# Third mixer's q,k convolution computed in the second mixer's stage

## The reference

```python
cqkv, gdnc1 = causal_conv(dqkv, gdnc0, prm['gdn_conv_w'][i])   # 4 taps along time
cqkv = jax.nn.silu(cqkv)
cq, ck, cv = jnp.split(cqkv, [GDN_H * GDN_DK, 2 * GDN_H * GDN_DK], axis=-1)
q = l2norm(heads(cq, GDN_H)) * GDN_DK ** -0.5
k = l2norm(heads(ck, GDN_H))
v = heads(cv, GDN_H)
```

## Time and profile before

| | |
|---|---|
| median of 3 runs | 2600.65 us (2597.46 to 2604.7) |
| profiled execution, its own time | 2596.66 us |
| span in its profile | 2594.9 us |
| PE busy | 2399.1 us (92%) |
| DVE, ACT, POOL busy | 1639.1 (63%), 1074.1 (41%), 181.1 (7%) |
| chain that ended last | PE 72%, DVE 17%, issue 6%, ACT 4% |

### The profile page before, as it was taken

The page is one execution under the profiler, slowest core; times in us unless marked ns, Lnnn a source line. Parts: engine busy times, 40 slices in busy tenths (PEclk is TensorE's granted clock), DMA queues, the critical chain, the costliest instruction groups (busy, mean ns, idle before and its releaser), DMA issues.

```text
span 2594.9 us, 38245 instructions
## 1 busy us (share of the span) xinstructions
PE 2399.1 (92%) x14436; PEld 2069.6 (80%) x14436; DVE 1639.1 (63%) x2112; ACT 1074.1 (41%) x1450; POOL 181.1 (7%) x247
## 2 busy tenths in 40 slices
PE   8899898899999899899798997999999999999996
PEld 6788778876899888789687866787887878878786
DVE  4554853743665454457636633778787887878776
ACT  4332311321333334324122220566666666667662
POOL 0212111201000001202012010000000000000000
PEclk8999898998999989999898988899999999999998
DMA  5323311322444333234112320898898978889871
GB/s 197 105 87 134 131 66 41 111 82 98 152 163 163 127 130 106 95 134 142 54 50 83 110 73 32 325 327 289 300 329 297 335 284 303 319 296 332 291 278 64
DMA packets 122566, 456.43 MB, mean 176 GB/s; under 512 B 14056, under 2 KB 14474, under 8 KB 120018
## 3 DMA queue, kind: packets, MB, share of 16 engines
q1 hardware_dynamic: 118818, 432.66, 47.5%
q0 software_dynamic: 3632, 22.12, 2.4%
HBM read 443.72 MB, written 11.00 MB: 175 GB/s over the span
## 4 chain that ended last, share of the span: by engine, by line
PE 72%; DVE 17%; issue 6%; ACT 4%; POOL 1%; DVEq 0%; DMA 0%; SPq 0%; ACTq 0%; POOLq 0%
PE ps L726 7%; PE ps L728 7%; PE ps L727 7%; PE ps L773 6%; DVE weights_low L2255 4%; PE ps L1293 4%; PE ps L1295 4%; PE ps L1294 4%; PE ps L1315 3%; PE ps L1316 3%; PE ps L1317 3%; PE ps L1266 3%; PE ps L767 2%; DVE arena L1889 2%; PE ps L808 1%
## 5 line engine op out<-in xcount | busy, mean ns | idle before, releaser
L726 PE MATMUL ps<-u_high,tiles_high 128*128 128x288 f32 x1688 | 526.0, 312 | 17.5 <-DVE tiles_low L1718 17.5
L727 PE MATMUL ps<-u_low,tiles_high 128*128 128x288 f32 x1688 | 513.0, 304 | 0.0
L728 PE MATMUL ps<-u_high,tiles_low 128*128 128x288 f32 x1688 | 511.1, 303 | 0.0
L1718 DVE TENSOR_TENSOR tiles_low<-ring,tiles_high 128x1024 fp32r<-128x1024 f32 x238 | 298.1, 1255 | 201.6 <-ACT tiles_high L1374 200.2
L726 PEld LDWEIGHTS ps<-u_high,tiles_high 128*128 128x128 f32 x1688 | 332.1, 197 | 26.7 <-issue 24.6
L2255 DVE TENSOR_TENSOR weights_low<-expert_ring,weights_high 128x1024 fp32r<-128x1024 f32 x288 | 334.5, 1219 | 5.2 <-ACT weights_high L1627 2.0
L727 PEld LDWEIGHTS ps<-u_low,tiles_high 128*128 128x128 f32 x1688 | 332.6, 197 | 0.5
L728 PEld LDWEIGHTS ps<-u_high,tiles_low 128*128 128x128 f32 x1688 | 332.2, 197 | 0.0
L1374 ACT ACTIVATE tiles_high<-ring 128x1024 fp32r<-128x1024 f32 x238 | 250.6, 1054 | 170.9 <-DMA ring<-in_stream 81.0
L1293 PE MATMUL ps<-weights_high,u_high 128*128 128x512 f32 (+1 forms) x768 | 297.6, 388 | 22.9 <-DVE weights_low L2255 22.3
L2255 DVE TENSOR_TENSOR weights_low<-ring,weights_high 128x1024 fp32r<-128x1024 f32 x240 | 280.2, 1218 | 43.2 <-ACT weights_high L1627 42.1
(11 more groups left out here) (381 smaller groups left out, 3290.2 us busy)
## 6 DMA issues: line engine op xcount, KB each, us to landing
ring<-in_stream SPq DMA_DIRECT2D x530, 512.0 KB, 4.2
expert_ring<-in_stream SPq DMA_DIRECT2D x288, 512.0 KB, 5.6
arena<-in_state POOLq DMA_DIRECT2D x8, 1024.0 KB, 5.1
state_s<-arena POOLq DMA_DIRECT2D x8, 1024.0 KB, 4.3
const<-in_const SPq DMA_DIRECT2D x1, 2052.5 KB, 12.0
arena<-in_const POOLq DMA_DIRECT2D x2, 832.0 KB, 4.9
h<-in_x SPq DMA_DIRECT2D x1, 1152.0 KB, 5.0
y<-acc POOLq DMA_DIRECT2D x1, 1152.0 KB, 4.4
```

Source lines behind the costliest of these rows:

```text
L726: mm(out, hi[k], uh[:, k, :], start=k == 0, stop=False)
L727: mm(out, hi[k], ul[:, k, :], start=False, stop=False)
L728: last = mm(out, lo[k], uh[:, k, :], start=False, stop=k == KD - 1)
L1718: tt(t_low[:, q % HELD, :], ring[:, (t % RING) * TILE:(t % RING + 1) * TILE], t_high[:, q % HELD, :].bitcast(F32), ALU.subtract).then_inc( ...
```

## The change

Blocks 0 to 3 of the third mixer's convolution (q and k) move into the second mixer's stage, with buffers of their own (`cbuf_early`, `ctan_early`) beside the retention's decay table. VectorE's `conv` is split into `conv_taps` and `conv_finish`, ScalarE's tanh into `conv_tanh`. The remaining four rounds of the third mixer now handle two slots each, the squares come first and the norm stands in the third of the four rounds. TensorE's sums of squares come after two slots instead of five. The convolution of the fourth mixer is written in the new functions with the same order as before.

The buffers, and TensorE's `gdn`:

```diff
+EARLY_CONV = 4
...
             ret_dec = carve(4 * PAIR)
+            cbuf_early = carve(640).rearrange("p (a c) -> p a c", a=2)
+            ctan_early = carve(640).rearrange("p (a c) -> p a c", a=2)
...
-                for s in range(5):
+                for s in range(2):
                     fill(L, GDN, s)
...
                 last.then_inc(qksum_ps, 1)
-                for s in range(5, 8):
+                for s in range(2, 8):
                     fill(L, GDN, s)
```

ScalarE's `core`, `out_norm` and the new `conv_gdn`:

```diff
                     fill(L, n, slot + hh)
+                    if n == RET and hh == 3:
+                        conv_tanh(L, GDN, 0)
                 if n != GLA:
                     take_o(HEADS[n] - 2)
                     take_o(HEADS[n] - 1)
+                if n == RET:
+                    conv_tanh(L, GDN, 1)
...
                 fill(L, n, slot)
+                if n == RET:
+                    conv_tanh(L, GDN, 2)
                 act.wait_ge(osum_ps, m + 1)
...
-                for s in range(slot + 1, NSLOT[n]):
+                fill(L, n, slot + 1)
+                if n == RET:
+                    conv_tanh(L, GDN, 3)
+                for s in range(slot + 2, NSLOT[n]):
                     fill(L, n, s)
...
+            def conv_gdn(L):
+
+                act.wait_ge(conv_ready, 14 * L + 4)
+                A(tmp4, cv[:, 0:4, :], ACT.Square).then_inc(qksq_ready, 1)
+                for i, b in enumerate(range(EARLY_CONV, NCONV[GDN])):
+                    if i > 0:
+                        fill(L, GDN, 2 * i - 2)
+                        fill(L, GDN, 2 * i - 1)
+                    conv_tanh(L, GDN, b)
+                    if b == 5:
                         act.wait_ge(qksum_ps, L + 1)
                         A(rs4, ps_t[:, M:M + 4, 0:TOK], ACT.Sqrt, bias=C("eps")).then_inc(qkrt_ready, 1)
+                fill(L, GDN, 6)
+                fill(L, GDN, 7)
```

VectorE's `scores`, `out_norm` (the first place there is behind the two gate products) and the new `conv_gdn`:

```diff
                     fill(L, n, slot + hh)
+                    if n == RET and hh >= 2:
+                        conv_taps(L, GDN, hh - 2)
+                        if hh == 3:
+                            conv_finish(L, GDN, 0)
...
+                if n == RET:
+                    conv_taps(L, GDN, 2)
+                    conv_finish(L, GDN, 1)
                 fill(L, n, slot)
                 dve.wait_ge(ort_ready, m + 1)
...
                 dve.wait_ge(o_final, m + 1)
+                if n == RET:
+                    conv_taps(L, GDN, 3)
+                    conv_finish(L, GDN, 2)
                 fill(L, n, slot + 1)
                 state(L, n)
+                if n == RET:
+                    conv_finish(L, GDN, 3)
                 for s in range(slot + 2, NSLOT[n]):
                     fill(L, n, s)
...
+            def conv_gdn(L):
+
+                for i, b in enumerate(range(EARLY_CONV, NCONV[GDN])):
+                    conv_taps(L, GDN, b)
+                    if i > 0:
+                        conv_finish(L, GDN, b - 1)
+                        fill(L, GDN, 2 * i - 2)
+                        fill(L, GDN, 2 * i - 1)
+                    if b == 6:
+                        qk_norm(L)
+                conv_finish(L, GDN, NCONV[GDN] - 1)
+                fill(L, GDN, 6)
+                fill(L, GDN, 7)
```

More of the change, by code:

```diff
@@ L1503, in decays, with conv_tanh, conv_ssd @@
                 A(egp[:, 0:q, :], egp[:, 0:q, :], ACT.Exp).then_inc(eg_ready, 1)
[L1505 to L1517, removed]
+            def conv_tanh(L, n, b):
+                c = 14 * L + CONV0[n] + b
+                act.wait_ge(convsum_ready, c + 1)
+                if c - 1 > 0:
+                    act.wait_ge(conv_ready, c - 1)
+                taps, t = scratch_of(n, b)
+                A(t[:, 0:312], taps[:, 0:312], ACT.Tanh).then_inc(ctan_ready, 1)
+            def conv_gdn(L):
[7 more added lines that the diff above has]
+                    if b == 5:
                         act.wait_ge(qksum_ps, L + 1)
                         A(rs4, ps_t[:, M:M + 4, 0:TOK], ACT.Sqrt, bias=C("eps")).then_inc(qkrt_ready, 1)
-                fill(L, n, NCONV[n] - 1)
+                fill(L, GDN, 6)
+                fill(L, GDN, 7)
+            def conv_ssd(L):
+                for b in range(NCONV[SSD]):
+                    if b > 0:
+                        fill(L, SSD, b - 1)
+                    conv_tanh(L, SSD, b)
+                fill(L, SSD, NCONV[SSD] - 1)
             def gla(L):
@@ L1925, in qk_norm @@
                 dve.wait_ge(qk_ready, L + 1)
-            def conv(L, n):
-                nb = NCONV[n]
-                wv = pv[:, PV["conv_w"][0]:PV["conv_w"][0] + 56].rearrange("p (k b) -> p k b", b=14)
[L1932 to L1960, removed]
@@ new lines, in conv_finish @@
+            def conv_finish(L, n, b):
+                dve.wait_ge(ctan_ready, 14 * L + CONV0[n] + b + 1)
+                c, t = scratch_of(n, b)
+                stt(cv[:, b, 0:256], t[:, 0:256], 1.0, c[:, 0:256], ALU.add, ALU.mult)
+                s7 = [q[:, 259:315].rearrange("p (s w) -> p s w", w=7)[:, :, 0:4] for q in (t, c)]
+                stt(cv[:, b, 256:288].rearrange("p (s w) -> p s w", w=4), s7[0], 1.0, s7[1],
+                    ALU.add, ALU.mult).then_inc(conv_ready, 1)
+                dve.wait_ge(conv_ready, 14 * L + CONV0[n] + b + 1)
@@ new lines, in conv_taps @@
+            def conv_taps(L, n, b):
+                wv = pv[:, PV["conv_w"][0]:PV["conv_w"][0] + 56].rearrange("p (k b) -> p k b", b=14)
+                ci = CONV0[n] + b
+                dve.wait_ge(stream_act, taken_before(T_OF[("z", L, n, b)] + 1, "act"))
+                dve.wait_ge(pads_ready, 2 * L + (1 if n == GDN else 2))
+                src = zblk(n, b)
+                out = scratch_of(n, b)[0][:, 0:312]
+                ts(out, src[:, 0:312], wv[:, 0, ci:ci + 1], PVc("conv_b", ci), ALU.mult, ALU.add).then_inc(dve_step, 1)
+                dve.wait_ge(dve_step, steps.next())
+                stt(out, src[:, 1:313], wv[:, 1, ci:ci + 1], out, ALU.mult, ALU.add).then_inc(dve_step, 1)
+                dve.wait_ge(dve_step, steps.next())
+                stt(out, src[:, 2:314], wv[:, 2, ci:ci + 1], out, ALU.mult, ALU.add).then_inc(dve_step, 1)
+                dve.wait_ge(dve_step, steps.next())
+                stt(out, src[:, 3:315], wv[:, 3, ci:ci + 1], out, ALU.mult, ALU.add).then_inc(convsum_ready, 1)
@@ L1962, in gla, with conv_ssd @@
+            def conv_ssd(L):
+                for b in range(NCONV[SSD]):
+                    conv_taps(L, SSD, b)
+                    if b > 0:
+                        conv_finish(L, SSD, b - 1)
+                        fill(L, SSD, b - 1)
+                conv_finish(L, SSD, NCONV[SSD] - 1)
+                fill(L, SSD, NCONV[SSD] - 1)
             def gla(L):
```

11 lines of the change are left out of this document (7 added, 4 removed).

## The result

The changed kernel takes a median of 2610.78 us (8 runs, 2609.73 to 2626.35); the kernel before, in runs beside it, 2599.15 us (8 runs, 2595.71 to 2604.70). The ratio is 1.006, with an interval of 1.0044 to 1.0075: **slower by 0.6%**, more than the 0.3% that a measurement can tell. The forecast was 2603.4 us, no change. The profiled executions differ by 13.3 us in span.

What follows compares the result with a forecast made beforehand. TensorE is busiest, so time counts only where it stands still or runs at half clock. Per layer +4.2, -0.2 and -2.65 give about +1.4; two layers +2.8 on 2600.65 make 2603.4 us, range 2594 to 2613.

Steps and rivals of the forecast that it cites:

- The wait of 10.1 us becomes 8.9 us in front of gate tile 6: Third mixer's head: TensorE's wait before the transposes moves to gate tile 6, behind norm and taps 7; 8.9 us.
- The reciprocal 1.7 us late, the end of the second mixer 4.2 late: Second mixer's end: VectorE and GpSimd contention delays the reciprocal 1.7 us; taps 3 and finish 2 add 2.65.
- Transposes at full clock, 2.65 us back: Third mixer: transposes take 2.18 us against 4.07, the next tile 4.08 against 4.86; -2.65 a layer.
- +1.4 us a layer, 1.0 to 1.8: Net per layer: +4.2 at the second mixer's end, -0.2 in the head, -2.65 in transposes and next tile.
- The sum: Whole kernel: two layers' net gives +2.8 us, 2603.4 us on the median's scale, no change.
- Half clock over two tiles: Rival: 0.50 clock holds beyond z tile 9 or gate tile 6, +2.7 us a layer and place; chance 0.17.
- The load with its drain: Rival: table switches ahead of gate tile 5's high half each add a 1.38 us drain; 2609 us, chance 0.03.
- the change does all it can: Rival: the 10.1 us wait and slow transposes vanish, only the 4.2 stay; -17 us, near 2583, chance 0.07.

Runs made afterwards that it cites:

- norm_behind: Changed kernel with the q,k norm moved behind the low halves of gate tiles 6 and 7; 2604.34 us, ratio 1.0026.
- split_norm: Changed kernel, taps 3 behind z tile 9's low half, norm halved: q before gate tile 5's low half, k behind tile 7's; 2568.48 us.
- layer0: The change made in layer 0 only, layer 1 in the order of the kernel before; 2611.24 us, ratio 1.0044.
- delay_l1: Kernel before plus a scratch reciprocal over two blocks (3.75 us) in front of layer 1's first norm; 2602.56 us, ratio 1.0012.
- delay: Kernel before plus a scratch reciprocal over two blocks in front of the third mixer's norm, both layers (3.8 us each); 2617.44 us, ratio 1.0066.
- after_d2: Changed kernel plus a scratch reciprocal (3.75 us) in front of layer 1's first norm; 2611.50 us, ratio 1.0044.

## Why the prediction was wrong

- **The wait of 10.1 us becomes 8.9 us in front of gate tile 6**: right. 8.56 us, in both layers, behind the norm and the taps of block 7, of which the first took 2.75 us beside GpSimd's copies: 2.3 over its usual 0.44, as forecast.
- **The reciprocal 1.7 us late, the end of the second mixer 4.2 late**: right, a little high. 1.2 us, and z tile 9 at 273.03 against 269.18, 3.85. The turns of VectorE and GpSimd came as counted: the second product ended near 255.1 (forecast 255.5). Two slips in the working change nothing: 1.7 + 2.65 is 4.35, not 4.2, and the pair of low halves at 253.20, of which two take 2.36 us elsewhere, ended at 257.27, behind the decays.
- **Transposes at full clock, 2.65 us back**: right. They took 2.13 us (323.41 to 325.54), against 4.07. Gate tiles 6 and 7 took 8.44 us, the forecast 8.4 to 9.1; the lower clock covered the first alone. Stretches at z tile 9 and at gate tiles 6 and 7 (columns as above), to be read against the earlier trace rows:

```profile
273.00:279.00 6.00, 5.97 (x27) 6.00 (x28) 5.21 (x6) 0.09 (x1) 1.12 (x2) 0.55 0.73 243
315.00:319.00 4.00, 4.00 (x17) 4.00 (x18) 1.40 (x3) 0.00 (x0) 0.00 (x0) 0.50 0.72 233
319.00:321.00 2.00, 2.00 (x15) 2.00 (x15) 0.00 (x0) 0.41 (x1) 0.00 (x0) 0.91 0.14 57
```

- **+1.4 us a layer, 1.0 to 1.8**: 0.2 in layer 0 and 0.1 in layer 1, below the bounds. Each of its terms was a little high: 3.9 at the end of the second mixer (forecast 4.2), -0.8 in the head (-0.2), -2.9 in the transposes and the tile behind (-2.65).
- **The sum** is the step that failed. It took twice the local term as the whole change: everything behind the head was to run as before, 3 us later. It did not. Of the 13.3 us, 3.0 arose between 335 and 650 us, 7.6 in the passage of layer 1 and 2.8 between 1260 and 1591, all in unchanged code, and in each of the three TensorE ran some 17 us more at the lower clock. The two edited stages took 0.2 and 0.1. So the local working holds to about a microsecond a layer, and the clock behind the stage has no term in it. That 2610.78 lies within the stated range, 2594 to 2613, owes nothing to this working: the upper part of the range stood for half clock over another tile of the edited stage, which did not come.
- *Rivals.* "Half clock over two tiles" named the right resource and the wrong place: at z tile 9 and at gate tile 6 it covered one. The load with its drain falls; ScalarE in the head of the changed kernel:

```profile
293.44 1.28 ACT L1542 ACT_TABLE_LOAD   x1
294.73 1.22 ACT L1542 ACTIVATE arena<-ps,const 128x1152 f32<-128x1152 f32 x1
295.97 1.28 ACT L1406 ACT_TABLE_LOAD   x1
297.27 0.41 ACT L1406 ACTIVATE arena<-ps 128x288 f32<-128x288 f32 x1
```

  Each load takes 1.28 us with the next instruction right behind. The drain of some 1.38 us for each switch of the Trainium skill ("ScalarE: Activation LUTs", What ACT_TABLE_LOAD costs) does not show.
- The rival "the change does all it can" was set aside because the low half of tile 6 stood behind the norm in the code. norm_behind and split_norm show that this order did hold it, but not alone: with the whole norm behind these low halves the transposes wait 4.77 us, with half of it 1.24.

*What the arrival is measured against.* Not the start of the execution: reckoned from there, an entry into layer 1's passage at 1084.48 us (layer0) drew 43.0 us and one at 1084.65 (delay_l1) 35.4; 1088.06 (delay) drew 43.0 and 1088.48 (after_d2) 35.4. The Trainium skill ("TensorE: Matmul & The Clock Gate", What's actually happening) says that what watches TensorE's activity runs freely and isn't reset when a kernel starts, which fits; no run here shows that watcher itself. But the traces show where its falls lie against the work. Shortly ahead of every passage, fast or slow, TensorE waits 1.14 us for VectorE, and some 3 us after that wait the clock falls, for 6.8 us. That wait and the fall, in the kernel before and in the changed one (the second line of each: columns as above; a clock of 0.71 over 1 us is a fall at 1070.4, one of 0.86 a fall at 1073.7):

```profile
1067.34 0.69 PE L1018 MATMUL ps<-arena,const 32*128 32x256 f32 x2 [1.14 <-DVE arena L2029]
1070.00:1071.00 1.00, 0.79 (x4) 0.48 (x3) 0.86 (x4) 0.00 (x0) 0.00 (x0) 0.71 0.15 57
```

```profile
1070.47 0.69 PE L1026 MATMUL ps<-arena,const 32*128 32x256 f32 x2 [1.14 <-DVE arena L2088]
1073.00:1074.00 1.00, 0.80 (x5) 0.42 (x4) 0.90 (x3) 0.00 (x0) 0.00 (x0) 0.86 0.27 107
```

In the 36 passages of the 18 profiles the fall comes 2.53 to 3.13 us after the wait's end in the 23 that took 35.4 us, and 3.19 to 3.34 us after it in the 13 that took 43.0 or 44.5, without an overlap. So which passage comes goes with where the work stands when the clock falls in front of it, and a few tenths of a microsecond make the difference.

*What stays open.* Why the clock falls again and again once it has fallen late, and what sets the place of the falls at the start of an execution. In layer 0, ahead of every edit, five of the 18 profiles drew the long passage, with the same code. No run set that place on purpose.

## What to carry to other kernels

A local sum can be right to a microsecond while the total is off by ten, when the engine that sets the pace has two clocks: before you put a loss down to the edit, lay the same instructions of both traces side by side and look where the lateness grows, and compare the time at the lower clock there. To tell an edit's cost from the clock's, run the old kernel with a pure delay, and the new one with a small one; if time and delay do not add up, judge the edit by the length of its own stage in the traces, not by the total. A line through time and mean clock doesn't price an edit that makes or removes a pause. A wait that an edit only moves is worth more work than the edit itself: the norm in two halves brought what moving the convolution had not.

## What the runs showed of the hardware

The passage took 35.4 us in some profiled executions and 43.0 in others (44.5 three times), and nothing between, in either layer and with the same instructions: a loss of 7.6 us (or 9.1) comes whole or not at all. Which of them came went with the place of the clock's last fall in front of the passage, 2.5 to 3.1 or 3.2 to 3.3 us after the same wait. In the changed kernel the clock fell within the passage in the middle of work, at 1087 us, after six microseconds in which TensorE was busy for 6.00 of 6.00 us at full clock; no idle time of over 0.2 us stood in front since 1073.5 us, and the clock had been at the lower level from 1073.7 to 1080.6. A delay of 1.95 us shortened a run by 5 us, and one of 7.4 us lengthened another by 19.8.
